# Scores of the first row tile of both attention branches: three products of rounded and low parts in place of one plain product

## The reference

```
s = jnp.einsum('bqhcd,bshcd->bhcqs', q_b, kb).astype(jnp.float32) * HEAD_DIM ** -0.5
causal = key_idx[None, :] <= t_b[:, None]
p = jax.nn.softmax(jnp.where(causal[None, None, None], s, -jnp.inf), axis=-1)
```

## Time and profile before

| | |
|---|---|
| median of 3 runs | 770.8 us (770.72 to 771.42) |
| profiled execution, whole | 771.19 us |
| its span, first to last instruction | 769.4 us |
| granted TensorE clock over the span | 1.000 |
| PE (TensorE matmul) busy | 765.3 us (99%) |
| PEld (TensorE weight load) busy | 644.5 us (84%) |
| DVE (VectorE) busy | 511.1 us (66%) |
| ACT (ScalarE) busy | 426.8 us (55%) |
| POOL (GpSimd) busy | 137.6 us (18%) |

### The profile page before, as it was taken

How to read it: one execution, slowest core, us unless ns; L and a number is a source line. 1 busy time by engine, 2 the same in 40 slices (tenths; PEclk the granted TensorE clock), 3 DMA queues, 4 the chain that set the end, 5 groups by cost and what they waited for, 6 DMA issues and landing times.

```text
span 769.4 us, 10401 instructions
## 1 busy us (share of the span) xinstructions
PE 765.3 (99%) x3576; PEld 644.5 (84%) x3576; DVE 511.1 (66%) x711; ACT 426.8 (55%) x693; POOL 137.6 (18%) x225
## 2 busy tenths in 40 slices
PE   9999999999999999999999999999999999999998
PEld 7899988888888888888888888888888888888887
DVE  6678788788776755678556565666465567765553
ACT  6865756676663745555656455455676334444331
POOL 4321533322221000000212222312110011110000
DMA  8988889988888665666866768767766887787553
GB/s 287 319 263 274 265 248 289 272 257 263 245 245 242 186 200 168 193 191 180 242 197 197 220 183 278 234 184 222 222 209 222 304 230 242 245 239 226 198 188 120
DMA packets 89613, 176.80 MB, mean 230 GB/s; under 512 B 7617, under 2 KB 15425, under 8 KB 89313
## 3 DMA queue, kind: packets, MB, share of 16 engines
q1 hardware_dynamic: 80752, 152.06, 64.8%
q0 software_dynamic: 8528, 23.87, 10.7%
q10 hardware_dynamic: 288, 0.30, 0.1%
HBM read 162.18 MB, written 14.02 MB: 229 GB/s over the span
## 4 chain that ended last, share of the span: by engine, by line
PE 99%; DMA 0%; DVE 0%; issue 0%
PE ps L742 29%; PE ps L744 29%; PE ps L743 29%; PE ps L756 1%; PE ps L760 1%; PE ps L776 1%; PE ps L777 1%; PE ps L766 1%; PE ps L842 0%; DMA xt<-in_x_columns 0%; PE ps L933 0%; PE ps L932 0%; PE ps L934 0%; PE ps L762 0%; PE ps L758 0%; PE ps L843 0%
## 5 line engine op out<-in xcount | busy, mean ns | idle before, releaser
L1285 DVE TENSOR_TENSOR lo<-raw,hi 128x1024 fp32r<-128x1024 f32 (+2 forms) x277 | 331.4, 1202 | 237.0 <-ACT hi L1008 235.8
L1008 ACT ACTIVATE hi<-raw 128x1024 fp32r<-128x1024 f32 (+2 forms) x277 | 286.2, 1038 | 300.2 <-PE ps L744 261.1
L742 PE MATMUL ps<-hi,hT_hi 128*128 128x512 f32 (+1 forms) x880 | 339.3, 386 | 0.0
L743 PE MATMUL ps<-lo,hT_hi 128*128 128x512 f32 (+1 forms) x880 | 339.0, 385 | 0.0
L744 PE MATMUL ps<-hi,hT_lo 128*128 128x512 f32 (+1 forms) x880 | 338.9, 385 | 0.0
L744 PEld LDWEIGHTS ps<-hi,hT_lo 128*128 128x128 f32 x880 | 165.2, 188 | 31.8
L742 PEld LDWEIGHTS ps<-hi,hT_hi 128*128 128x128 f32 x880 | 165.2, 188 | 31.7
L743 PEld LDWEIGHTS ps<-lo,hT_hi 128*128 128x128 f32 x880 | 165.2, 188 | 31.3
L742 PE MATMUL ps<-hi,ogT_hi 128*128 128x512 f32 x128 | 49.8, 389 | 0.0
L743 PE MATMUL ps<-lo,ogT_hi 128*128 128x512 f32 x128 | 49.8, 389 | 0.0
L744 PE MATMUL ps<-hi,ogT_lo 128*128 128x512 f32 x128 | 49.8, 389 | 0.0
(11 more groups left out here) (192 smaller groups left out, 654.3 us busy)
## 6 DMA issues: line engine op xcount, KB each, us to landing
raw<-in_w_in SPq DMA_DIRECT2D x190, 512.0 KB, 4.4
raw<-in_w_out SPq DMA_DIRECT2D x32, 512.0 KB, 4.6
raw<-in_w_o_a SPq DMA_DIRECT2D x16, 512.0 KB, 5.4
raw<-in_w_o_b SPq DMA_DIRECT2D x16, 512.0 KB, 4.2
raw<-in_w_in SPq DMA_DIRECT2D x16, 384.0 KB, 5.1
turned<-swapped POOLq DMA_DIRECT2D x12, 512.0 KB, 3.3
v<-turned POOLq DMA_DIRECT2D x32, 128.0 KB, 5.5
raw<-in_w_in SPq DMA_DIRECT2D x7, 336.0 KB, 4.5
```

The lines of the kernel that those rows point to most:

```text
L742: mm(o, a_hi, w_hi[:, j], start=first and j == 0, stop=False)
L743: mm(o, a_hi, w_lo[:, j], start=False, stop=False)
L1008: activation(hi[:, slot, :, 0:width], raw[:, slot, :, 0:width], ACT.Copy).then_inc(hi_ready, 1)
L1285: tt(lo[:, slot, :, 0:width], raw[:, slot, :, 0:width], hi[:, slot, :, 0:width].bitcast(F32), ALU.subtract).then_inc(lo_ready, 1)
```

## The change

`qk_scores` computes the first row tile's scores as three products of rounded and low parts, each 128 columns wide, into the same accumulator, in place of the one plain product. For this the first row tile's queries are now written rounded, with low parts of their own, which take the place of the plain keys in `m_r` (columns 384 to 511 of each map); the plain copy of the keys goes. ScalarE's `qkT_out` so has two copies for every group. VectorE's `qk_lo_out` has two subtractions for every group.

```
-        K_LO, Q_LO, K_FIRST = slice(0, S), slice(S, S + P), slice(S + P, CW)
-        K_LO_0, K_LO_1 = slice(0, P), slice(P, S)
+        K_LO, K_LO_0, K_LO_1 = slice(0, S), slice(0, P), slice(P, S)
+        Q_LO_0, Q_LO_1 = slice(S + P, CW), slice(S, S + P)
...
                 o = ps[:, bank, P:P + S]
-                mm(ps[:, bank, 0:P], qkT[:, q_block, 0:P], of_map(t, K_FIRST, m), start=True, stop=True)
+                first = ps[:, bank, 0:P]
+                mm(first, qk_hi[:, q_block, 0:P], qk_hi[:, k_block, 0:P], start=True, stop=False)
+                mm(first, qk_hi[:, q_block, 0:P], of_map(t, K_LO_0, m_r), start=False, stop=False)
+                mm(first, of_map(t, Q_LO_0, m_r), qk_hi[:, k_block, 0:P], start=False, stop=True)
                 mm(o, qk_hi[:, q_block, P:S], qk_hi[:, k_block, :], start=True, stop=False)
                 mm(o, qk_hi[:, q_block, P:S], of_map(t, K_LO, m_r), start=False, stop=False)
-                mm(o, of_map(t, Q_LO, m_r), qk_hi[:, k_block, :], start=False, stop=True).then_inc(scores, 1)
+                mm(o, of_map(t, Q_LO_1, m_r), qk_hi[:, k_block, :], start=False, stop=True).then_inc(scores, 1)
...
-                if is_query(n):
-                    activation(by_blocks(of_blocks(n, slice(P, S), qk_hi)), columns_of(1), ACT.Copy)
-                    ins = activation(by_blocks(of_blocks(n, slice(0, P), qkT)), columns_of(0), ACT.Copy)
-                else:
-                    for r in range(RT):
-                        activation(by_blocks(of_blocks(n, slice(r * P, (r + 1) * P), qk_hi)), columns_of(r), ACT.Copy)
-                    ins = activation(by_blocks(of_four(n, K_FIRST, m)), columns_of(0), ACT.Copy)
+                for r in range(RT):
+                    ins = activation(by_blocks(of_blocks(n, slice(r * P, (r + 1) * P), qk_hi)), columns_of(r), ACT.Copy)
                 ins.then_inc(qkT_ready, 1)
...
-                for r, part in ((1, Q_LO),) if is_query(n) else enumerate((K_LO_0, K_LO_1)):
+                for r, part in enumerate((Q_LO_0, Q_LO_1) if is_query(n) else (K_LO_0, K_LO_1)):
                     rounded = by_blocks(of_blocks(n, slice(r * P, (r + 1) * P), qk_hi)).bitcast(F32)
                     ins = tt(by_blocks(of_four(n, part, m_r)), columns_of(r), rounded, ALU.subtract)
```

## The result

| | before | after |
|---|---|---|
| median | 771.31 us (13 runs, 770.72 to 772.92) | 772.92 us (13 runs, 772.65 to 773.95) |
| profiled execution, whole | 771.19 us | 772.66 us |
| its span | 769.4 us | 770.9 us |
| granted TensorE clock | 1.000 | 1.0 |

The changed kernel is slower: the ratio of after to before is 1.0024, with a 95% interval of 1.0017 to 1.0031. That is +1.6 us between the medians, and 1.3 to 2.4 us by the interval. Forecast were 772.6 us and +1.8. (The 770.8 us that the prediction started from is the median of the first 3 of these 13 runs.)

What follows compares the result with a forecast made beforehand. TensorE, working back to back, was taken to bound the kernel. Three narrow turns in 16 calls gave +1.8 us, the other terms nothing, so 770.8 + 1.8 = 772.6 us, range 771.6 to 778.4.

Steps and rivals of the forecast that it cites:

- What bounds the kernel: Whole kernel: TensorE works back to back, busy 99% of the span, so added work on it is added to the end.
- Term 1: TensorE in the scores: three narrow products of 0.11 us replace a plain one of 0.22 us, 16 calls, +1.8 us.
- The bound by the load: Scores on TensorE: a 128x128 load of rounded or low parts takes 0.10 to 0.11 us, so narrow products cost at least that.
- The 81 ns that spoke against the sum: Skill's figure for a sustained load and matmul pair 128 columns wide; three would take 0.24 us, the term +0.4 us.
- Term 2: ScalarE in the key groups: one plain copy fewer, 2.5 us less work, worth nothing at the end.
- Term 3: VectorE's `qk_lo_out` in the query groups: a second subtraction, 2.7 us more work, hidden by its lead and counted at nothing.
- The rival of the thin cover: VectorE in the query groups: the ring runs empty, +2.7 us on top of +1.8, 775.3 us; chance 0.04.
- Term 4: After the scores: `masked_max` gets its semaphore 0.11 us later, bank reuse is units away; costs nothing.
- The range: Whole kernel's predicted time, 771.6 to 778.4 us, taking in the forecast and the plain pace.
- Plain pace: Scores on TensorE: each narrow product takes the plain product's 0.22 us, +7.0 us, 777.8 us; chance 0.34.
- Overlapping loads: Scores on TensorE: the new products' loads overlap, turns of 0.06 to 0.07 us, -0.4 us, 770.4 us; chance 0.06.
- The forecast case: Scores on TensorE: each narrow product's turn is 0.11 us, +1.8 us, 772.6 us; chance 0.56.

## Why the prediction was right, and where not

**What bounds the kernel: right.** TensorE's stream has no slack behind the first call. Six narrow turns in place of the plain product, 16 x (0.66 - 0.22) = 7.0 us, came out as +7.2 and +7.4 us, in two kernels that reached them in different ways.

**Term 1, three turns of 0.11 us: right, in size and in cause.** The call grew from 0.58 to 0.69 us, and 16 x 0.11 = 1.8 stands against +1.6 between the medians and +1.9 in the trace. The bound by the load, taken from pairs of loads in the first products, was shown to be the cause: the turn stayed at 0.11 us for 64, 128 and (0.12) 256 moving columns, and fell to 0.06 with half the stationary ones. The load in question is that of the product behind, which the prediction's reading implies and doesn't say. The estimate of 0.06 us for streaming 128 columns, a quarter of 0.23, was right too; it shows only when the load is out of its way.

**The 81 ns that spoke against the sum: wrong here.** The loads of 128 columns around the scores start no closer than 0.11 us apart in every kernel here (in the earlier trace rows one pair is at 0.10, where the prediction says 0.11 at the least), and those of 64 columns 0.06. By the Trainium skill (TensorE: Matmul & The Clock Gate, section "LDWEIGHTS (loading the stationary operand)") it is columns divided by 1.2, an estimated 107 and 53 ns; the trace agrees with the first, and 0.06 is a little above the second, where the streaming of 128 columns bounds as well. The 81 ns of its section "Back-to-back issue gap" for a sustained stream 128 wide doesn't hold for these operands of rounded and low parts: 0.11 us was measured.

**Term 2, ScalarE, nothing: right.** TensorE's part undone, with ScalarE's and VectorE's kept, left 1.0001 (0.9992 to 1.0010).

**Term 3, VectorE, nothing: the outcome was right, the reason mis-sized.** "up to three units, some 8 us, before TensorE needs it" was a wrong step. I took the depth of the ring for the cover, from VectorE's mean load and its waiting for ScalarE over the whole span, and did not ask how full the ring is in that stretch; the line of ScalarE's waits for DMA, 32.9 us, was passed over. About 2 us are left there in the mean, and in two executions TensorE waited for low parts as it was. The added 0.685 us mostly fits under it, so the term stays nothing within the interval, but by a margin some four times smaller than the one it was argued from, and in that the outcome was partly luck. The rival of the thin cover was nearer than the 0.04 it got: with 2.2 us more in each group it begins.

**Term 4: right.** PE has no wait between the calls.

**The range.** By its own terms the lower end is 770.8 + 1.3 - 0.4 = 771.7 us, not 771.6. Nothing hangs on it.

**The rivals.** Plain pace (777.8 us), given 0.34, was wrong: one load and one matmul for each narrow product, 0.11 us, not 0.22. Overlapping loads (770.4 us) was wrong: L843 and L844 keep the same stationary operand, and both loads take their full turn.

**Same or slower.** The forecast case stood close to the line of 0.2%. The ratio 1.0024 lies beyond it, but the interval (1.0017 to 1.0031) reaches to both sides: that the kernel is slower is clear, that it is so by over 0.2% is not.

## What to carry to other kernels

In a stream of products without a wait, a product here took the longer of two times: its own streaming, and the load of the product behind it. For rounded and low parts a load of 128 columns is 0.11 us. So at 128 moving columns three products cost 0.33 us against 0.22 for one plain product, while at 256 columns each costs nearly the same 0.12 and does twice the work. Whether three products then beat a plain one of 256 columns is not shown, since no kernel here has a plain product that wide. Below 256 columns count loads, not columns. And measure how far ahead a ring is in the stretch that a change touches: its depth says how far it could be, the waits there on DMA say how far it is.

## What I had not expected of the hardware

A long wait could be followed by a slower clock. In the kernel with eight extra subtractions PE waited 1.96 us until 149.65, and from 150.56 its 512-column products followed each other every 0.43 us instead of 0.23, some 3 us long. The timeline of PE, and the busy time of that stretch (us, PE, PEld, DVE, ACT, POOL, PEclk):

```profile
149.65 0.50 PE L742 MATMUL ps<-hi,hT_hi 128*128 128x512 f32 x1 [1.96 <-DVE lo L1283]
...
150.56 0.63 PE L742 MATMUL ps<-hi,hT_hi 128*128 128x512 f32 x1
150.99 0.63 PE L743 MATMUL ps<-lo,hT_hi 128*128 128x512 f32 x1
...
153.12 0.63 PE L742 MATMUL ps<-hi,hT_hi 128*128 128x512 f32 x1
```
```profile
150.30:153.40 3.10, 3.10 (x9) 2.45 (x8) 1.56 (x2) 0.00 (x0) 2.94 (x4) 0.50 0.87 241
```

The granted clock was 0.50 there, the 1.2 GHz level; it is 1.00 before (149.65 to 150.30) and after (156 to 170). The six products from 150.56 to 153.12 took 2.56 us, where at 0.23 us each they would have taken 1.4. The same happened behind two more waits, and did not happen behind two others:

```profile
127.51 0.50 PE L742 MATMUL ps<-hi,hT_hi 128*128 128x512 f32 x1 [1.77 <-DVE lo L1283]
194.13 0.50 PE L742 MATMUL ps<-hi,hT_hi 128*128 128x512 f32 x1 [3.41 <-DVE lo L1283]
260.13 0.47 PE L742 MATMUL ps<-hi,hT_hi 128*128 128x512 f32 x1 [2.07 <-DVE lo L1283]
278.97 0.50 PE L742 MATMUL ps<-hi,hT_hi 128*128 128x512 f32 x1 [2.64 <-DVE lo L1283]
```
```profile
194.70:197.90 3.20, 3.20 (x9) 2.52 (x8) 3.19 (x3) 1.33 (x4) 3.12 (x2) 0.50 0.93 282
280.20:283.50 3.30, 3.30 (x9) 2.56 (x9) 3.17 (x5) 0.00 (x0) 0.00 (x0) 0.51 0.81 227
```

Behind the waits of 1.77 and 2.07 us the products kept their 0.23 us. So the length of the wait alone doesn't decide it: 1.96 us was followed by the lower clock and 2.07 was not. Over the whole span of 794.0 us the granted clock was 0.994, which is an estimated 10 us at 0.50 in place of 1.00, and a loss of some 5 us of the 24.6. These 5 us are not VectorE's time but TensorE's at half its clock. That the waits brought the clock down is read from their order alone; no run here tried it by itself.
